# Strassen's scheme in the MLP of a two-block network: product order, order of the queues, and the engine that sums the quarters of u

## The chip, the cores and the metric

One core of a Trainium2 chip runs the whole network. The metric is the device time of one execution in microseconds (us), the median of several runs.

## The reference

The network has a first block (attention and a state-space mixer, one layer) and a second block of two layers, each a mixer followed by an MLP. The MLP is all that the change touches. It works on 512 tokens, with 1024 model columns and 4096 hidden columns:

```python
h = _rms_norm_2(x, g_pre_mlp[l])
y = jnp.square(jax.nn.relu(h @ w_up[l])) @ w_down[l]
x = x + _rms_norm_2(y, g_post_mlp[l])
```

All is float32. The kernel gets near float32 precision out of matmuls of rounded operands: each operand is split into a high part (a copy rounded to fp32r) and a low part (the operand minus the high part), and each product takes three matmuls, high by high, high by low, and low by high.

## The kernel before

The hidden columns are cut into 32 units of 128. `up(f)` makes unit f: 24 matmuls of 512 columns, then ACT takes the relu out of PSUM and squares it (`unit_done`). The result is called u.

The down product (u times `w_down`) of the first 24 units is done by a scheme of Strassen's: two units make a pair, and a 2x2 block product is made of 7 products instead of 8. The left side has four quarters of u (A11, A12, A22 in `U_ALL`, A21 in `A21_`) and four sums of them (S1 to S4, also in `U_ALL`). The right side has four quarters of the weights (B11, B21, B22 and B12) and four sums (T1 to T4, in `T_ALL`). One step is one pair against one half of the output columns: 7 products of 6 matmuls each, 42 matmuls of 256 columns. The last 8 units go the plain way.

The stage runs in 6 rounds a layer (d = 0 to 5), and each of the two layers has this stage. PE's order in round d is: step 0 (pair 2d), step 1 (pair 2d+1), `up(4d+5)`, step 2 (pair 2d), step 3 (pair 2d+1), `up(4d+6)`, `up(4d+7)`, `up(4d+8)`. The pair that step 1 needs is complete when `up(4d+3)` is, which is the last but one unit ahead of step 0 of the same round.

What is prepared for a step, and where:

- the sums T1 to T4 of the weights: DVE, `step_sums` (L531 to L533)
- high parts of the weights' quarters and of T: ACT, `step_hi` (L520, L521 for the quarters, then L523 for T, behind a wait for DVE's sums)
- low parts: DVE, `step_lo` (L540, L541) and `step_lo_sums` (L548)
- the sums S1 to S4 of u: POOL (L2701 to L2704, four operations on 128x256)
- high parts of u: ACT, `pair_hi` (L2320, the first 768 columns: A11, A12, A22) and `pair_hi_sums` (L2325, the 1024 columns of S1 to S4)
- low parts of u: POOL (L2708, two operations, of 768 and of 1024 columns)
- high and low part of the weights of `up`: ACT `up_hi` (L479) and DVE `up_lo` (L485)

A step on PE begins with two waits: for both low parts of the pair's u (`u_pool`), and for all parts of the step's weights (`w_lo`). The results of the products are added up on DVE by `collect` (L2564, L2567, out of PSUM) in seven tiles Z; at the end of the last round seven additions of 128x1024 (`plus`, L2594) make the output of them. Every engine works its queue in the order in which it is written; engines wait for one another by counting semaphores. `dve_link` and `pool_link` make an engine wait for its own operation just issued. The weights come by DMA in a ring of 8 slots, in PE's order, and a slot is loaded again when PE is done with it.

Of the kernel before, what the change touches and what calls it, by code (L numbers as in the profile page):

```python
# [62 lines left out]
def up_number(f):  # L63

    if f < 4:
        return J_MLP + f
    if f >= 4 * NST + 4:
        return J_LATE + f - 4 * NST - 4
    d, r = divmod(f - 4, 4)
    return J_MLP + 4 + 12 * d + (0, 3, 8, 11)[r]  # L70


def step_number(n):

    return J_MLP + 4 + 12 * (n // 4) + (1, 4, 6, 9)[n % 4]
# [9 lines left out]
PRODUCTS = ((A11, B11), (A12, B21), (S4, B22), (A22, T4), (S1, T1), (S2, T2), (S3, T3))  # L85
# [104 lines left out]
def build(nc, a, out, first=True, second=True):  # L190
# [20 lines left out]
    with ExitStack() as ctx:  # L211
# [76 lines left out]
        Z = [carve(A0, 2, 512), quarter(0, 0), quarter(0, 1), quarter(1, 0), quarter(1, 1), carve(A0 + 1024, 2, 512), carve(A0 + 2048, 2, 512)]  # L288
# [1890 lines left out]
        def two_act(act, l, post_gain):  # L2179
# [116 lines left out]
            def unit_done(f):  # L2296
# [13 lines left out]
                if p >= 2:  # L2310
                    act.wait_ge(sem.u_pool, N_POOL * l + 2 * (p - 2) + 1)
# [82 lines left out]
        def two_dve(dve, l):  # L2394
# [173 lines left out]

            for d in range(NST):
                if d:  # L2570
                    collect(d - 1, 1, range(7))
# [4 lines left out]
                up_lo(dve, l, 4 * d + 5)
                step_sums(dve, l, 4 * d + 1)
                step_lo(dve, l, 4 * d + 1)
                step_lo_sums(dve, l, 4 * d + 1)
# [70 lines left out]
        def two_pool(pool, l):  # L2650
# [286 lines left out]
```

## Time and profile before

| | |
|---|---|
| median of 3 runs | 1773.59 us (1771.93 to 1783.68) |
| profiled execution | 1772.09 us, span of its instructions 1770.0 us |
| mean granted clock of TensorE | 0.979 of full speed |
| PE busy | 1672.6 us, 94% of the span |
| DVE busy | 1114.7 us, 63% |
| ACT busy | 713.6 us, 40% |
| POOL busy | 564.8 us, 32% |

PE is TensorE's matmuls, DVE is VectorE, ACT is ScalarE, POOL is GpSimd. L and a number is a line of the kernel. The time of an execution is its span and some 2 us around it. A line of a timeline gives the start, the duration, the engine, the line, the operation, what it writes and reads, and, in brackets, how long the engine was idle before it and for whom it waited. A duration there reaches from the start of an operation to its end, and holds the time in which the operation itself was held up.

### The profile page before, as it was taken

The page shows a single profiled execution, that of the slowest core. Times are in us where ns is not written, and L with a number is a line of the kernel's source. Part 1 is how long each engine was busy: PE and PEld are TensorE (multiplying, and loading weights), DVE is VectorE, ACT ScalarE, POOL GpSimd, SP SyncE. Part 2 cuts the span into 40 slices and gives each one's busy share as a digit, 9 for nine tenths or more (in the row PEclk, how much of TensorE's full clock was granted, in tenths as well). Part 3 has the DMA queues.
Part 4 walks back from the last instruction along what each step waited for, and adds up shares of the span by engine and source line. Part 5 has one row for each costly group of instructions (what it writes and reads, how often), then busy time and mean ns, then how long its engine had stood idle before and what let it go on. Part 6 is the DMA issues. An engine that isn't in the chain of part 4 may idle for free.

```text
span 1770.0 us, 25358 instructions
## 1 busy us (share of the span) xinstructions
PE 1672.6 (94%) x9563; PEld 1303.7 (74%) x9563; DVE 1114.7 (63%) x1955; ACT 713.6 (40%) x1426; POOL 564.8 (32%) x594
## 2 busy tenths in 40 slices
PE   7989999999999999899999999999999989999998
PEld 4555456487866679888888778887667978888876
DVE  6999666345447735677777563444773577777754
ACT  3233342342346635443443244234672543343321
POOL 1010001231126635333333632112663533333360
PEclk9999999999999999999999999899999999999999
DMA  6324220145220005232323234422000522332321
GB/s 189 66 26 99 67 95 1 39 143 143 58 87 1 1 15 142 84 96 84 96 88 92 83 74 127 124 50 95 2 1 4 152 84 86 93 96 84 95 84 48
DMA packets 195019, 136.91 MB, mean 77 GB/s; under 512 B 34487, under 2 KB 176562, under 8 KB 194898
## 3 DMA queue, kind: packets, MB, share of 16 engines
q1 hardware_dynamic: 188604, 128.07, 24.8%
q10 hardware_dynamic: 6294, 7.22, 1.8%
q8 instruction: 77, 1.26, 0.3%
q14 instruction: 44, 0.36, 0.1%
HBM read 131.00 MB, written 2.10 MB: 75 GB/s over the span
## 4 chain that ended last, share of the span: by engine, by line
PE 73%; DVE 15%; ACT 4%; issue 3%; POOL 3%; DMA 2%; ACTq 0%; POOLq 0%; DVEq 0%; SPq 0%
PE ps L563 13%; PE ps L564 13%; PE ps L565 12%; PE ps L2115 4%; PE ps L2117 4%; PE ps L2116 4%; PE ps L1999 4%; PE ps L2015 3%; PE ps L2030 3%; PE ps L1199 3%; POOL U_LO L2708 1%; PE ps L1887 1%; DMA WR<-in_cmp_w_v 1%; PE ps L605 1%; DVE BIG L2594 1%
## 5 line engine op out<-in xcount | busy, mean ns | idle before, releaser
L565 PE MATMUL ps<-HT_R,WR_R 128*128 128x512 f32 (+1 forms) x832 | 314.1, 377 | 0.0
L563 PE MATMUL ps<-HT_R,UP_HI 128*128 128x512 f32 x448 | 178.7, 399 | 6.7 <-DVE WR_R L485 6.7
L565 PEld LDWEIGHTS ps<-HT_R,WR_R 128*128 128x128 f32 x832 | 157.5, 189 | 31.9
L564 PE MATMUL ps<-HL_MLP,UP_HI 128*128 128x512 f32 x448 | 178.0, 397 | 0.0
L485 DVE TENSOR_TENSOR WR_R<-WR,UP_HI 128x1024 fp32r<-128x1024 f32 x56 | 82.7, 1477 | 144.0 <-ACT UP_HI L479 143.9
L2187 ACT ACTIVATE BIG<-ps 64x512 f32<-64x512 f32 (+3 forms) x124 | 71.7, 580 | 180.7 <-PE ps L565 161.8
L2512 DVE CUSTOM_DVE_ANT_0 ps<-ps,tri 128x512 f32<-128x512 f32 (+1 forms) x192 | 93.1, 502 | 57.3 <-PE ps L1999 56.6
L2287 ACT ACTIVATE BIG<-ps,mn 128x512 f32<-128x512 f32 (+1 forms) x192 | 100.3, 528 | 59.9 <-DVE mn L2512 53.1
L2682 POOL TENSOR_SCALAR BIG<-BIG,rg,gate 128x512 f32<-128x512 f32 (+3 forms) x128 | 76.7, 613 | 149.2 <-DVE rg L2528 148.9
L2115 PE MATMUL ps<-H,U_HI 128*128 128x256 f32 x288 | 86.8, 301 | 39.5 <-POOL U_LO L2708 29.6
L2708 POOL TENSOR_TENSOR U_LO<-BIG,U_HI 128x768 fp32r<-128x768 f32 (+1 forms) x48 | 107.8, 2258 | 31.3 <-ACT U_HI L2325 29.4
L893 PE MATMUL ps<-WR,HT 128*128 128x512 f32 (+1 forms) x256 | 114.0, 596 | 1.2 <-ACT BIG L1676 1.2
L2115 PE MATMUL ps<-WH_MLP,U_HI 128*128 128x256 f32 x384 | 110.8, 289 | 0.0
L2116 PE MATMUL ps<-WH_MLP,U_HI 128*128 128x256 f32 x384 | 110.4, 288 | 0.0
L2117 PE MATMUL ps<-WH_MLP,U_LO 128*128 128x256 f32 x384 | 110.1, 287 | 0.0
L2701 POOL TENSOR_TENSOR BIG<-BIG 128x256 f32<-128x256 f32 x24 | 18.2, 759 | 287.6 <-ACT BIG L2308 287.6
L523 ACT ACTIVATE WH_MLP<-BIG 128x1024 fp32r<-128x1024 f32 x48 | 51.0, 1062 | 143.8 <-DVE BIG L533 143.8
L563 PEld LDWEIGHTS ps<-HT_R,UP_HI 128*128 128x128 f32 x448 | 85.0, 190 | 26.6 <-issue 7.5
L2567 DVE TENSOR_TENSOR BIG<-ps,BIG 128x512 f32<-128x512 f32 x140 | 93.4, 686 | 14.8 <-PE ps L2117 13.0
L564 PEld LDWEIGHTS ps<-HL_MLP,UP_HI 128*128 128x128 f32 x448 | 85.0, 190 | 18.6
L1999 PE MATMUL ps<-BIG 64*128 64x384 f32 (+7 forms) x384 | 96.9, 474 | 1.6 <-ACT BIG L2287 1.0
L564 PE MATMUL ps<-WR_R,HT_R 128*128 128x512 f32 (+1 forms) x256 | 95.0, 371 | 0.0
(398 smaller groups left out, 4304.2 us busy)
## 6 DMA issues: line engine op xcount, KB each, us to landing
WR<-in_w_up SPq DMA_DIRECT2D x64, 512.0 KB, 4.0
WR<-in_w_down SPq DMA_DIRECT2D x96, 256.0 KB, 3.3
WR<-in_w_in SPq DMA_DIRECT2D x36, 512.0 KB, 5.4
WR<-in_w_out SPq DMA_DIRECT2D x6, 2048.0 KB, 7.8
WR<-in_w_in SPq DMA_DIRECT2D x5, 2048.0 KB, 8.3
WR<-in_w_down SPq DMA_DIRECT2D x16, 512.0 KB, 3.6
WR<-in_cmp_w_k SPq DMA_DIRECT2D x2, 2048.0 KB, 8.2
WR<-in_cmp_w_v SPq DMA_DIRECT2D x2, 2048.0 KB, 8.2
```

What stands on the lines that cost most here:

```text
L563: nc.tensor.matmul(out_, w[0], x[0], start=start, stop=False)
L564: nc.tensor.matmul(out_, w[0], x[1], start=False, stop=False)
L565: return nc.tensor.matmul(out_, w[1], x[0], start=False, stop=stop)
L893: last = nc.tensor.matmul(ps[bank][:, 0:width], HT[:, k, P * m:P * m + P], wv[:, k, 0:width], start=(k == 0), stop=(k == KD - 1))
L1999: nc.tensor.matmul(s_bank(u, o)[:, 0:P * (t + 1)], q_of(kind, h, t), k_of(kind, h, P * (t + 1)), start=True, stop=True).then_inc(sem.s_ps, 1)
L2115: nc.tensor.matmul(out_, x[0], w[0], start=(i == 0 and t == 0), stop=False, skip_group_check=True)
L2116: nc.tensor.matmul(out_, x[0], w[1], start=False, stop=False, skip_group_check=True)
L2117: last = nc.tensor.matmul(out_, x[1], w[0], start=False, stop=(i == 1), skip_group_check=True)
L2287: nc.scalar.activation(PR[u % 3][:, o, 0:w], s_bank(u, o)[:, 0:w], ACT.Exp, bias=mn[:, i:i + 1], scale=-1.0, accum_out=rs[:, 2 * u + o:2 * ...
L2512: nc.vector.tensor_tensor_reduce(s_bank(u, o)[:, 0:w], s_bank(u, o)[:, 0:w], tri[:, SEQ - w:SEQ], 1.0, 3.0e38, ALU.add, ALU.min, mn[:, i:i ...
L2567: nc.vector.tensor_tensor(z, src, z, ALU.add).then_inc(sem.z_sum, 1)
L2708: last = nc.gpsimd.tensor_tensor(U_LO[p % 3][:, cols_], U_ALL[p % 3][:, cols_], U_HI[p % 3][:, cols_].bitcast(F32), ALU.subtract)
```

## The change

- Products: A22 by T4 comes third and S4 by B22 fourth (they change places), and the tiles Z are named to match.
- PE: the wait at the head of a step asks only for the first low part of u (A11, A12, A22) and for the low parts of the weights' quarters. The wait for T's low part stands ahead of the third product, the wait for the low part of S1 to S4 ahead of the fourth. POOL signals its two low parts one by one.
- S1 to S4 are computed by DVE (`pair_sums`) instead of POOL, in the same four operations. They stand between `step_lo_sums(4d)` and `step_sums(4d+1)` for the odd pair, between `step_lo_sums(4d+3)` and `up_lo(4d+7)` for the even one, and ahead of `step_sums(0)` for the first. They are counted by `t_sum`, which ACT and POOL now wait for.
- ACT: `up_hi(4d+5)` goes behind `step_hi(4d+1)` and `pair_hi_sums(2d+1)`. DVE: `up_lo(4d+5)` goes behind the sums and low parts of step 4d+1.
- End of the last round on DVE: the seven `plus` in another order, and `up_lo(28)` to `up_lo(31)` between them: 4 `plus`, 28, 1 `plus`, 29, 1 `plus`, 30, 1 `plus`, 31. Before: 28, 5 `plus`, 29, 2 `plus`, 30, 31.

```diff
-PRODUCTS = ((A11, B11), (A12, B21), (S4, B22), (A22, T4), (S1, T1), (S2, T2), (S3, T3))
+PRODUCTS = ((A11, B11), (A12, B21), (A22, T4), (S4, B22), (S1, T1), (S2, T2), (S3, T3))
...
             def strassen_step(d, sweep, i):
 
                 n, p = 4 * d + 2 * sweep + i, 2 * d + i
-                pe.wait_ge(sem.u_pool, N_POOL * l + 2 * p + 2)
-                pe.wait_ge(sem.w_lo, NSPLIT * l + step_number(n) + 2)
+                pe.wait_ge(sem.u_pool, N_POOL * l + 2 * p + 1)
+                pe.wait_ge(sem.w_lo, NSPLIT * l + step_number(n) + 1)
                 for q, (left, right) in enumerate(PRODUCTS):
                     if i == 0:
                         product_bank_free(d, sweep, q)
+                    if q == 2:
+                        pe.wait_ge(sem.w_lo, NSPLIT * l + step_number(n) + 2)
+                    if q == 3:
+                        pe.wait_ge(sem.u_pool, N_POOL * l + 2 * p + 2)
...
             def pair_hi_sums(p):
 
-                act.wait_ge(sem.u_pool, N_POOL * l + 2 * p + 1)
+                act.wait_ge(sem.t_sum, N_SUM * l + pair_sum_number(p))
...
                 pair_hi(2 * d + 1)
-                up_hi(act, l, c + 1)
                 step_hi(act, l, 4 * d + 1)
                 pair_hi_sums(2 * d + 1)
+                up_hi(act, l, c + 1)
                 unit_done(c)
...
+            def pair_sums(p):
+
+                part = lambda i: U_ALL[p % 3][:, 256 * i:256 * i + 256]
+                dve.wait_ge(sem.u_act, N_ACT * l + 5 * p + 3)
+                dve_link(nc.vector.tensor_tensor(part(S1), A21_[:, p % 2, :], part(A22), ALU.add))
+                dve_link(nc.vector.tensor_tensor(part(S2), part(S1), part(A11), ALU.subtract))
+                nc.vector.tensor_tensor(part(S3), part(A11), A21_[:, p % 2, :], ALU.subtract)
+                nc.vector.tensor_tensor(part(S4), part(A12), part(S2), ALU.subtract).then_inc(sem.t_sum, 1)
+
             for d in range(NST):
                 if d:
                     collect(d - 1, 1, range(7))
                 up_lo(dve, l, 4 * d + 4)
+                if d == 0:
+                    pair_sums(0)
                 step_sums(dve, l, 4 * d)
                 step_lo(dve, l, 4 * d)
                 step_lo_sums(dve, l, 4 * d)
-                up_lo(dve, l, 4 * d + 5)
+                pair_sums(2 * d + 1)
                 step_sums(dve, l, 4 * d + 1)
                 step_lo(dve, l, 4 * d + 1)
                 step_lo_sums(dve, l, 4 * d + 1)
+                up_lo(dve, l, 4 * d + 5)
...
+                if d + 1 < NST:
+                    pair_sums(2 * d + 2)
                 up_lo(dve, l, 4 * d + 7)
             collect(NST - 1, 1, range(7))
-            up_lo(dve, l, F_PLAIN + 4)
             dve.wait_ge(sem.z_sum, z_count(l, NST - 1, 1, 6))
             plus(1, 0)
-            plus(2, 4)
+            plus(3, 4)
             dve_link(plus(5, 0))
-            plus(2, 5)
+            plus(3, 5)
+            up_lo(dve, l, F_PLAIN + 4)
             dve_link(plus(6, 5))
             up_lo(dve, l, F_PLAIN + 5)
-            dve_link(plus(3, 6))
+            dve_link(plus(2, 6))
+            up_lo(dve, l, F_PLAIN + 6)
             dve_link(plus(4, 6))
-            for f in range(F_PLAIN + 6, NF):
-                up_lo(dve, l, f)
+            up_lo(dve, l, F_PLAIN + 7)
...
             for p in range(NPAIR):
-                pool.wait_ge(sem.u_act, N_ACT * l + 5 * p + 3)
-                pool_link(nc.gpsimd.tensor_tensor(part(S1), A21_[:, p % 2, :], part(A22), ALU.add))
-                pool_link(nc.gpsimd.tensor_tensor(part(S2), part(S1), part(A11), ALU.subtract))
-                nc.gpsimd.tensor_tensor(part(S3), part(A11), A21_[:, p % 2, :], ALU.subtract)
-                nc.gpsimd.tensor_tensor(part(S4), part(A12), part(S2), ALU.subtract).then_inc(sem.u_pool, 1)
-                pool.wait_ge(sem.u_pool, N_POOL * l + 2 * p + 1)
+                pool.wait_ge(sem.t_sum, N_SUM * l + pair_sum_number(p))
                 for n, cols_ in enumerate((slice(0, 768), slice(768, 1792))):
                     pool.wait_ge(sem.u_act, N_ACT * l + 5 * p + 4 + n)
-                    last = nc.gpsimd.tensor_tensor(U_LO[p % 3][:, cols_], U_ALL[p % 3][:, cols_], U_HI[p % 3][:, cols_].bitcast(F32),
-                                                   ALU.subtract)
-                last.then_inc(sem.u_pool, 1)
+                    nc.gpsimd.tensor_tensor(U_LO[p % 3][:, cols_], U_ALL[p % 3][:, cols_], U_HI[p % 3][:, cols_].bitcast(F32),
+                                            ALU.subtract).then_inc(sem.u_pool, 1)
```

## Rows read from the trace of the kernel before

**Rows 1.** Waits of PE over the whole span: us in total, times, longest us
```profile
PE ps L2115 <- POOL U_LO L2708: 29.6, 10, 3.0
PE ps L2115 <- DVE WH_MLP L548: 9.9, 2, 5.0
...
PE ps L563 <- DVE WR_R L485: 6.7, 2, 3.4
```

**Rows 2.** Busy time by stretch; its columns are in the first line
```profile
core 0: us, PE busy (x) PEld busy (x) DVE busy (x) ACT busy (x) POOL busy (x), PEclk, DMA share, GB/s
725.80:735.80 10.00, 10.00 (x86) 10.00 (x85) 6.50 (x8) 4.09 (x5) 8.12 (x6) 1.00 0.36 107
735.80:752.50 16.70, 16.70 (x74) 13.51 (x73) 7.53 (x11) 7.90 (x13) 3.38 (x4) 1.00 0.34 95
702.40:985.10 282.70, 262.92 (x1585) 235.75 (x1583) 207.98 (x251) 112.33 (x167) 108.63 (x78) 0.97 0.30 90
1411.90:1694.80 282.90, 263.14 (x1585) 236.04 (x1583) 208.01 (x251) 112.37 (x167) 108.58 (x78) 0.97 0.30 90
752.50:798.10 45.60, 42.64 (x265) 38.15 (x264) 33.61 (x43) 19.94 (x30) 16.65 (x13) 1.00 0.32 93
798.10:845.20 47.10, 44.14 (x265) 39.66 (x264) 33.79 (x43) 20.05 (x30) 16.66 (x13) 0.96 0.30 90
712.50:720.20 7.70, 7.70 (x43) 7.70 (x44) 6.42 (x11) 2.01 (x2) 0.00 (x0) 0.62 0.00 0
988.50:990.50 2.00, 1.98 (x5) 1.61 (x6) 1.97 (x2) 0.00 (x0) 1.92 (x2) 0.50 0.00 0
```

**Rows 3.** Timeline of PE, start of the second step of round 1
```profile
760.64 0.39 PE L2115 MATMUL ps<-H,U_HI 128*128 128x256 f32 x1 [2.96 <-POOL U_LO L2708]
```

**Rows 4.** Timeline of ACT, round 1 of layer 0
```profile
748.25 0.63 ACT L2308 ACTIVATE BIG<-relu 128x512 f32<-128x512 f32 x1
748.91 0.85 ACT L2320 ACTIVATE U_HI<-BIG 128x768 fp32r<-128x768 f32 x1
...
756.06 1.06 ACT L523 ACTIVATE WH_MLP<-BIG 128x1024 fp32r<-128x1024 f32 x1 [4.52 <-DVE BIG L533]
757.03 1.04 ACT L2325 ACTIVATE U_HI<-BIG 128x1024 fp32r<-128x1024 f32 x1
```

**Rows 5.** Timeline of DVE, round 1 of layer 0
```profile
747.77 1.23 DVE L548 TENSOR_TENSOR WH_MLP<-BIG,WH_MLP 128x1024 fp32r<-128x1024 f32 x1
...
753.61 1.96 DVE L532 TENSOR_TENSOR BIG<-WR,BIG 128x256 f32<-128x256 f32 x1
755.60 0.42 DVE L533 TENSOR_TENSOR BIG<-WR,BIG 128x256 f32<-128x256 f32 x1
...
757.15 1.23 DVE L548 TENSOR_TENSOR WH_MLP<-BIG,WH_MLP 128x1024 fp32r<-128x1024 f32 x1
...
772.10 1.22 DVE L548 TENSOR_TENSOR WH_MLP<-BIG,WH_MLP 128x1024 fp32r<-128x1024 f32 x1
```

**Rows 6.** Timeline of POOL, round 1 of layer 0
```profile
748.96 0.74 POOL L2701 TENSOR_TENSOR BIG<-BIG 128x256 f32<-128x256 f32 x1 [13.31 <-ACT BIG L2308]
...
753.10 2.19 POOL L2708 TENSOR_TENSOR U_LO<-BIG,U_HI 128x768 fp32r<-128x768 f32 x1
758.14 2.44 POOL L2708 TENSOR_TENSOR U_LO<-BIG,U_HI 128x1024 fp32r<-128x1024 f32 x1 [2.86 <-ACT U_HI L2325]
```

**Rows 7.** Timeline of ACT, second square of round 0
```profile
692.00 0.63 ACT L2308 ACTIVATE BIG<-relu 128x512 f32<-128x512 f32 x1
```

**Rows 8.** Timeline of DVE, low parts of round 0's second step
```profile
708.99 3.37 DVE L548 TENSOR_TENSOR WH_MLP<-BIG,WH_MLP 128x1024 fp32r<-128x1024 f32 x1
```

**Rows 9.** Timeline of POOL, first unit after the pairs, round 5
```profile
945.95 1.48 POOL L2714 TENSOR_TENSOR BIG<-BIG 128x512 f32<-128x512 f32 x1
```

**Rows 10.** Timeline of DVE, final sums of the products
```profile
976.76 9.63 DVE L2594 TENSOR_TENSOR BIG<-BIG 128x1024 f32<-128x1024 f32 x5
986.42 1.95 DVE L485 TENSOR_TENSOR WR_R<-WR,UP_HI 128x1024 fp32r<-128x1024 f32 x1
```

More of the change, by code:

```diff
@@ L58 @@
 N_ACT, N_POOL = 5 * NPAIR + NF - F_PLAIN, 2 * NPAIR + NF - F_PLAIN
+N_SUM = NSTEP + NPAIR
 J_LATE, J_DOWN = J_MLP + 4 + 12 * NST, J_MLP + 8 + 12 * NST
@@ L69, in up_number, with step_sum_number, pair_sum_number @@
     d, r = divmod(f - 4, 4)
-    return J_MLP + 4 + 12 * d + (0, 3, 8, 11)[r]
+    return J_MLP + 4 + 12 * d + (0, 5, 8, 11)[r]
 def step_number(n):
-    return J_MLP + 4 + 12 * (n // 4) + (1, 4, 6, 9)[n % 4]
+    return J_MLP + 4 + 12 * (n // 4) + (1, 3, 6, 9)[n % 4]
+def step_sum_number(n):
+    return 6 * (n // 4) + (1, 3, 4, 5)[n % 4] + 1
+def pair_sum_number(p):
+    return 3 * p - p % 2 + 1
 def relu_number(f):
@@ L287, in build @@
         quarter = lambda t, half: Y[:, 2 * t:2 * t + 2, 512 * half:512 * half + 512]
-        Z = [carve(A0, 2, 512), quarter(0, 0), quarter(0, 1), quarter(1, 0), quarter(1, 1), carve(A0 + 1024, 2, 512), carve(A0 + 2048, 2, 512)]
+        Z = [carve(A0, 2, 512), quarter(0, 0), quarter(1, 0), quarter(0, 1), quarter(1, 1), carve(A0 + 1024, 2, 512), carve(A0 + 2048, 2, 512)]
         HL_IN = [carve(17408, KD, SEQ), parts("HL_IN", at_BIG + 4 * 17408, KD, SEQ)]
@@ L521, in step_hi @@
             nc.scalar.activation(H2[i][:], WR[:, u.slot, 512:1024], ACT.Copy).then_inc(sem.w_hi, 1)
-            act.wait_ge(sem.t_sum, NSTEP * l + n + 1)
+            act.wait_ge(sem.t_sum, N_SUM * l + step_sum_number(n))
             nc.scalar.activation(WH_MLP[2 * i + 1][:], T_ALL[i], ACT.Copy).then_inc(sem.w_hi, 1)
@@ L537, in step_lo @@
             u, i = by_name[f"st{n}_{l}"], n % 2
-            dve.wait_ge(sem.t_sum, NSTEP * l + n + 1)
+            dve.wait_ge(sem.t_sum, N_SUM * l + step_sum_number(n))
             dve.wait_ge(sem.w_hi, NSPLIT * l + step_number(n) + 1)
@@ L2310, in unit_done @@
                 if p >= 2:
-                    act.wait_ge(sem.u_pool, N_POOL * l + 2 * (p - 2) + 1)
+                    act.wait_ge(sem.t_sum, N_SUM * l + pair_sum_number(p - 2))
                 if p >= 3:
@@ L2698, in two_pool @@
             for p in range(NPAIR):
-                part = lambda i: U_ALL[p % 3][:, 256 * i:256 * i + 256]
-                pool.wait_ge(sem.u_act, N_ACT * l + 5 * p + 3)
-                pool_link(nc.gpsimd.tensor_tensor(part(S1), A21_[:, p % 2, :], part(A22), ALU.add))
-                pool_link(nc.gpsimd.tensor_tensor(part(S2), part(S1), part(A11), ALU.subtract))
-                nc.gpsimd.tensor_tensor(part(S3), part(A11), A21_[:, p % 2, :], ALU.subtract)
-                nc.gpsimd.tensor_tensor(part(S4), part(A12), part(S2), ALU.subtract).then_inc(sem.u_pool, 1)
-                pool.wait_ge(sem.u_pool, N_POOL * l + 2 * p + 1)
+                pool.wait_ge(sem.t_sum, N_SUM * l + pair_sum_number(p))
                 for n, cols_ in enumerate((slice(0, 768), slice(768, 1792))):
                     pool.wait_ge(sem.u_act, N_ACT * l + 5 * p + 4 + n)
-                    last = nc.gpsimd.tensor_tensor(U_LO[p % 3][:, cols_], U_ALL[p % 3][:, cols_], U_HI[p % 3][:, cols_].bitcast(F32),
-                                                   ALU.subtract)
-                last.then_inc(sem.u_pool, 1)
+                    nc.gpsimd.tensor_tensor(U_LO[p % 3][:, cols_], U_ALL[p % 3][:, cols_], U_HI[p % 3][:, cols_].bitcast(F32),
+                                            ALU.subtract).then_inc(sem.u_pool, 1)
             for f in range(F_PLAIN, NF):
```

## The prediction

> **What bounds the kernel now.** I read the share of busy time first: PE is busy 94% of the span, the next engine 63%. So a gain can only come out of PE's idle time, or out of time in which PE runs at its low clock. The waits of PE say how much of it the change can reach [rows 1]: 29.6 us for POOL's low parts of u in 10 places, 9.9 us for a low part of T in 2 places, 6.7 us for the low part of an `up` weight in 2 places. That is 46.2 us. The third view is the table of stretches [rows 2]. It shows what the waits cost beyond themselves. Two steps without a wait between take 10.0 us and three `up` units 16.7 us, so a round of four steps and four units is worth 10.0 + 5.6 + 10.0 + 16.7 = 42.3 us (42.4 with the digits that the cut takes off). Round 1 takes 45.6 us with a wait of 3.0 us. Round 2 takes 47.1 us with the same wait: its granted clock is 0.96. The step behind the 5.0 us wait takes 7.7 us instead of 5.0, at a granted clock of 0.62. Half speed is TensorE's lower level, 1.2 instead of 2.4 GHz, and in each of these places PE had been idle just before the clock was down. So the waits are paid a second time.
>
> The whole prize: from the first step to the end of `up(28)` layer 0 takes 282.7 us and layer 1 282.9 us, against 6 x 42.4 = 254.4 us. That is 28.3 + 28.5 = 56.8 us. Behind it comes the wait of 3.4 us for `up_lo(29)` in each layer, with a clock of 0.50 in the 2 us after it [rows 1, 2], worth some 1.2 us more: 2 x 4.6 = 9.2 us. Together 66 us can be had at most.
>
> **Why PE waits in a round.** Times are from the start of round 1's step 0 at 752.5. The square that completes pair 3 ends at -3.6 [rows 4]. POOL starts the sums 0.1 us later, and is done with its first low part at +2.8. Its second waits until +5.6 for ACT, and ends at +8.1 [rows 6]; PE starts step 1 there, 3.0 us late [rows 3]. ACT was late because its copy of T stands ahead of the copy of S and waited for DVE's last sum of T, done at +3.5 [rows 4, 5]. DVE was late because `up_lo(4d+5)` stood ahead of these sums, and because it was held: a sum of 256 columns takes 0.42 us, but the one at 753.61 took 1.96 us. It ended at 755.57, 0.3 us behind the end of POOL's operation that began at 753.10 [rows 5, 6]. Operations of DVE and POOL that read two SBUF tensors keep each other out.
>
> **The change part by part.**
>
> *The sums of u on DVE.* Four operations of 0.42 us with two links between are 1.7 us; POOL took 0.74 us for one alone and 4.1 us for all (748.96 to 753.10). DVE is free at -3.5 (L548 ends at 749.0 [rows 5]) and the square is there, so nothing is waited for: sums done at -1.8. DVE goes on with the first sum of T (0.7 us), to -1.2. POOL's first low part takes 1.9 us alone, until +0.7. DVE's other two sums end at +1.6. ACT's copies of T and of S (1.06 and 1.04 us) end at +2.7 and +3.6. DVE's `step_lo` ends at +2.5 and `step_lo_sums` (1.23 us) at +3.9. POOL's second low part waits for this and takes 2.44 us: +6.4 instead of +8.1.
>
> *The waits inside the step.* Step 1 may begin at +5.0. It needs the first low part (+0.7) and the quarters' (+2.5). A product takes 5.0 / 7 = 0.72 us: the third comes at +6.4 and needs T (+3.9), the fourth at +7.2 and needs +6.4. So no wait is left, by a margin of 0.8 us. Added waits that are met already cost nothing that can be seen: a step with a wait in front of every product and one with none take 10.0 us together, 84 matmuls at an even pace [rows 2]. If the pair's part had to be complete at the head, as before, 1.4 us would remain.
>
> *`up_hi` and `up_lo(4d+5)` later.* ACT makes the high part until +4.7, DVE the low part when POOL lets go, +6.4 to +7.6; PE needs it at +10.0.
>
> *What is late next.* PE comes 3.1 us earlier to the later steps, DVE doesn't. Before, the last low part of step 3 was ready at 773.3, +20.8 [rows 5]; in the new order `step_sums(4d+2)` ends at +9.2 in place of +9.5, so it comes at +20.5. Step 3 now begins at 10.0 + 5.6 + 5.0 = +20.6 and wants T at +22.0. It fits, by 1.5 us. The even pair's sums (1.7 us) follow on DVE at +20.5, ahead of `up_lo(4d+7)` (ready about +25.8 with POOL in between, wanted at +31.2) and of the seven sums of products, whose first is wanted at +31.2 and done near +26.4. In round 5 POOL also has the unit behind the pairs: it asks for the port as soon as the pair is done (1.48 us for its first operation [rows 9], three operations in all). This can push DVE back 2 to 3 us, so that step 3 there waits 1 us: -1 us a layer.
>
> *Round 0.* The square of pair 0 ends at 692.6 [rows 7]. The same walk gives the second low part of u at 702.6, in time for step 0 at 702.4. Then ACT has two units to square (2.5 us), DVE starts pair 1's sums behind POOL at 702.6, and the parts for step 1 come at 708.7 (quarters), 710.1 (T; before, 712.4 [rows 8]), 712.5 (low part of S). PE is ready at 707.4: it waits 1.3 us at the head and 1.7 us at the fourth product. For the clock I take 1.5 us, as behind the 3.0 us wait of round 2 (bounds 0 and 2.7, the rows of rounds 1 and 0). This leaves 4.5 us a layer.
>
> *The end.* Five `plus` took 9.63 us, 1.93 each, and `up_lo(29)` stood behind them (986.42 to 988.37, PE ready at 985.1) [rows 10]. With four ahead of `up_lo(28)`, DVE starts them 0.9 us after step 3's end and does `up_lo(28)` 9.8 us after it; PE wants it at 11.2. `up_lo(29)` is done by 14.5 and wanted at 16.8; the later ones wait for ACT as before. The wait goes, with its clock: 4.6 us a layer.
>
> Sum: 56.8 + 9.2 - 2 x 4.5 - 2 x 1 = 55 us. Profiled execution: 1772.1 - 55 = 1717. The median of before is 1.5 us above it: 1718.5 us.
>
> **A rule against the row.** The gap between 1.96 and 0.42 us for one and the same sum is what I put down to POOL. The Trainium skill, Advanced Engine Details, section "VectorE Performance Modes", lets only DVE's 2-port modes clash with POOL, and these sums (float32, two SBUF inputs) would not be among them; the same skill's SBUF — State Buffer, section "Who interferes with whom", says that two SBUF inputs are enough, and the row sides with that. By the first rule alone the sums of round 0's step 1 would not be held, which is the first rival below.
>
> **The rivals.**
>
> *No exclusion.* What the row shows is then chance. In round 0 the sums would end at 703.9 and the second low part of u at about 710.0, wanted at 709.5: 0.5 us in place of 4.5, and none in round 5. 8 + 2 us less: 1708.5. The row speaks against it, and so do its neighbours. 4%.
>
> *The second low part of u misses the fourth product.* My margin there is 0.8 us in a chain of ten operations and handovers. If POOL is let in one operation of DVE later (1.2 us), or two, each of the 10 rounds keeps 0.5 to 1.5 us, in half of them with 1 us of clock: 10 to 20 us given back, 1728 to 1739. 24%.
>
> *DVE becomes the bound, and it is slower.* DVE is busy 33.6 us of round 1 [rows 2]; 3.4 us come on top, and POOL's two low parts of both pairs, 8.6 us, shut out its SBUF work: 45.6 us at worst against the 42.4 that PE wants. At both `pair_sums` it also stands still until ACT's square, with `step_sums` or `collect` queued behind, and PE waits for those. At 1.5 us for each stand the round takes 48.6 us, 2 more than the present mean of some 46.6: 11 rounds, +22 us, 1795. It decides from stands of 0.5 us on. Against it: the 33.6 holds time in which DVE was held by POOL already, and its sums out of PSUM (L2567) do not read two SBUF tensors. 3%.
>
> *The time is given back at step 2 or 3.* If the later steps' parts are as late as before and PE only meets them sooner, the 3.1 us move to step 3. My walk has 1.5 us of margin at T. If it is wrong by 3, only the end and round 0 gain: 1760. 7%.
>
> **How the numbers follow.** Forecast 1718.5, 58%, own range 1708 to 1726 (clock of round 0 between its bounds, the 2 us of round 5 gone or doubled). A measurement here tells about 1% from nothing. With 4% left for what I see no case for (half of it between 1739 and 1756), faster by over 1% (below 1755.9) holds 0.89, within 1% 0.07, slower 0.04. For 8 in 10 the range takes in the better rival and the misses of the fourth product: 1706 to 1740.
>
> **What would show it.** Right: no wait of PE for L2708's successor in rounds 1 to 5; rounds of 42.4 us; a wait of about 3 us in two parts at round 0's step 1; S1 to S4 on DVE at 0.42 us each when POOL is still; no wait for `up_lo(29)`; DVE's busy time up by 24 x 1.7 = 41 us less what it was held before, POOL's down by up to 24 x 4.1 = 98 us. Wrong: a wait ahead of the fourth product in every round (second rival), PE waiting at steps 2 and 3 for `step_lo_sums`, or a first low part of u that does not begin until DVE's sums of T are done and pushes the second behind +7.2.

## The result and the profile after

The changed kernel takes 1714.25 us (median of 4 runs, 1707.73 to 1719.12) against 1772.76 us (4 runs, 1768.89 to 1783.68): a ratio of 0.9658, 95% interval 0.9604 to 0.9712. The forecast was 1718.5 us. The profiled execution took 1707.73 us, 64.4 us less than that of before; its span is 1705.8 us. It is the fastest of the four executions of the changed kernel, while the profiled one of before lies near its median; so the medians differ by less, 58.5 us.

PE's idle time first, from the page of the changed kernel (line of engines):

```profile
PE 1649.0 (97%) x9563; PEld 1283.3 (75%) x9563; DVE 1127.8 (66%) x2051; ACT 711.0 (42%) x1426; POOL 482.5 (28%) x498
```

and PE's waits in it (us in total, times, longest us). The step's matmuls are now at L2130 to L2132, `up` at L574 to L576:

```profile
PE ps L2130 <- POOL U_LO L2731: 2.1, 2, 1.1
...
PE ps L2130 <- DVE WR_R L552: 0.5, 2, 0.3
```

These are all the waits in the steps that PE's list still shows. The 29.6, 9.9 and 6.7 us of [rows 1] have become 2.1 and 0.5 us, all in round 0. The table of stretches, for the six rounds of each layer up to `up(28)`, rounds 1 and 2, the first two steps of round 0, and the units and last additions behind the rounds:

```profile
core 0: us, PE busy (x) PEld busy (x) DVE busy (x) ACT busy (x) POOL busy (x), PEclk, DMA share, GB/s
702.30:958.10 255.80, 254.47 (x1585) 228.45 (x1584) 217.85 (x296) 112.77 (x170) 72.70 (x34) 1.00 0.34 99
1379.50:1635.30 255.80, 254.47 (x1585) 228.50 (x1584) 217.89 (x296) 112.77 (x170) 72.64 (x34) 1.00 0.34 99
746.40:788.70 42.30, 42.30 (x265) 38.05 (x264) 35.49 (x51) 19.77 (x30) 9.90 (x5) 1.00 0.34 100
788.70:831.10 42.40, 42.40 (x266) 38.08 (x266) 35.57 (x51) 19.77 (x30) 10.01 (x5) 1.00 0.34 100
702.30:714.10 11.80, 10.47 (x86) 10.09 (x85) 10.85 (x14) 6.51 (x12) 4.70 (x2) 1.00 0.29 89
941.40:974.90 33.50, 33.50 (x146) 27.02 (x145) 19.70 (x17) 8.69 (x11) 23.08 (x15) 1.00 0.31 94
```

The six rounds take 255.8 us in place of 282.7 and 282.9 [rows 2]. Rounds 1 and 2 take 42.3 and 42.4 us, all of it busy, at full clock: 45.6 and 47.1 before, and the 42.4 us that four steps and four units are worth. The granted clock is 1.00 in every row: in this execution the low clock went with the waits. That is the smaller part of the gain. PE's waits in the steps and for `up_lo(29)` fell by 46.2 - 2.6 = 43.6 us; in the stretch defined below, which was 63.6 us shorter, PE was also busy 20.1 us less, with the same matmuls.

The chain that used to be late, in round 1 (step 0 begins at 746.42). DVE:

```profile
742.82 0.43 DVE L2588 TENSOR_TENSOR BIG<-BIG 128x256 f32<-128x256 f32 x1
743.28 0.42 DVE L2589 TENSOR_TENSOR BIG<-BIG 128x256 f32<-128x256 f32 x1
743.74 0.42 DVE L2590 TENSOR_TENSOR BIG<-BIG 128x256 f32<-128x256 f32 x1
744.08 0.42 DVE L2591 TENSOR_TENSOR BIG<-BIG 128x256 f32<-128x256 f32 x1
744.41 0.69 DVE L542 TENSOR_TENSOR BIG<-WR 128x512 f32<-128x512 f32 x1
745.13 1.95 DVE L543 TENSOR_TENSOR BIG<-WR,BIG 128x256 f32<-128x256 f32 x1
747.12 0.42 DVE L544 TENSOR_TENSOR BIG<-WR,BIG 128x256 f32<-128x256 f32 x1
...
748.67 1.23 DVE L559 TENSOR_TENSOR WH_MLP<-BIG,WH_MLP 128x1024 fp32r<-128x1024 f32 x1
```

ACT and POOL:

```profile
742.15 0.63 ACT L2323 ACTIVATE BIG<-relu 128x512 f32<-128x512 f32 x1
...
747.58 1.06 ACT L534 ACTIVATE WH_MLP<-BIG 128x1024 fp32r<-128x1024 f32 x1 [3.09 <-DVE BIG L544]
748.54 1.05 ACT L2340 ACTIVATE U_HI<-BIG 128x1024 fp32r<-128x1024 f32 x1
```

```profile
744.58 2.23 POOL L2731 TENSOR_TENSOR U_LO<-BIG,U_HI 128x768 fp32r<-128x768 f32 x1 [12.74 <-DVE BIG L2591]
749.66 2.50 POOL L2731 TENSOR_TENSOR U_LO<-BIG,U_HI 128x1024 fp32r<-128x1024 f32 x1 [2.86 <-ACT U_HI L2340]
```

DVE begins the sums of u as soon as the square has ended (742.78), has them at 744.50, goes on with T's first sum, and its second (745.13) is held until POOL's first low part lets go: 1.95 us, as in [rows 5]. POOL's second low part ends at 752.16, 5.7 us after the start of step 0. The fourth product of step 1 wants it at 7.2.

Read over both layers, the time from the first matmul of step 0 of round 0 to the first matmul of the plain down product fell from 304.3 + 304.6 = 608.9 us to 272.65 + 272.67 = 545.3 us: 63.6 of the 64.2 us of span. I call this the MLP stretch below. It is the sharper measure: in the profiles of all kernels here this stretch began between 699.2 and 711.4 us after the start, with the same instructions ahead of it, while the two layers of one profile agree within 0.1 us where no low clock falls, and within 1.6 us elsewhere. It rests on one profiled execution of each kernel, so for kernels with low clock in it a difference of some 2 us says nothing.

### The profile page after: what moved, and what is told of

Same layout as the page of the kernel before. It is cut to its first block, busy times and chain, and to the rows that moved or that the text cites. A ratio compares the mean times of both kernels' runs of the same rounds, so it can differ in the third digit from the quotient of the medians.

```text
span 1705.8 us, 25404 instructions
## 1 busy us (share of the span) xinstructions
PE 1649.0 (97%) x9563; PEld 1283.3 (75%) x9563; DVE 1127.8 (66%) x2051; ACT 711.0 (42%) x1426; POOL 482.5 (28%) x498
## 4 chain that ended last, share of the span: by engine, by line
PE 79%; DVE 13%; issue 2%; ACT 2%; DMA 2%; POOL 2%; ACTq 0%; DVEq 0%; POOLq 0%; SPq 0%
PE ps L574 14%; PE ps L575 14%; PE ps L576 14%; PE ps L2130 4%; PE ps L2131 4%; PE ps L2132 4%; PE ps L2010 4%; PE ps L2026 3%; PE ps L2041 3%; PE ps L1210 3%; PE ps L1898 1%; DMA WR<-in_cmp_w_v 1%; PE ps L616 1%; PE ps L1118 1%; PE ps L1199 1%
## 5 line engine op out<-in xcount | busy, mean ns | idle before, releaser
L576 PE MATMUL ps<-HT_R,WR_R 128*128 128x512 f32 (+1 forms) x832 | 313.3, 377 | 0.0
L2731 POOL TENSOR_TENSOR U_LO<-BIG,U_HI 128x768 fp32r<-128x768 f32 (+1 forms) x48 | 118.2, 2472 | 357.3 <-DVE BIG L2591 317.3
L576 PEld LDWEIGHTS ps<-HT_R,WR_R 128*128 128x128 f32 x832 | 156.9, 189 | 31.7
L574 PE MATMUL ps<-HT_R,UP_HI 128*128 128x512 f32 x448 | 177.3, 396 | 0.0
L496 DVE TENSOR_TENSOR WR_R<-WR,UP_HI 128x1024 fp32r<-128x1024 f32 x56 | 106.3, 1898 | 80.3 <-ACT UP_HI L490 79.1
L2131 PE MATMUL ps<-WH_MLP,U_HI 128*128 128x256 f32 x384 | 108.3, 282 | 0.0
L2132 PE MATMUL ps<-WH_MLP,U_LO 128*128 128x256 f32 x384 | 108.3, 282 | 0.0
L2130 PE MATMUL ps<-WH_MLP,U_HI 128*128 128x256 f32 x384 | 108.3, 282 | 0.0
L574 PEld LDWEIGHTS ps<-HT_R,UP_HI 128*128 128x128 f32 x448 | 84.2, 188 | 19.0
L904 PEld LDWEIGHTS ps<-WR,HT 128*128 128x128 f32 x256 | 48.5, 194 | 56.0 <-issue 54.5
L2582 DVE TENSOR_TENSOR BIG<-ps,BIG 128x512 f32<-128x512 f32 x140 | 87.0, 677 | 0.0
L2130 PE MATMUL ps<-H,U_HI 128*128 128x256 f32 x288 | 81.4, 283 | 2.7 <-POOL U_LO L2731 2.1
```

The source lines that it names most:

```text
L496: nc.vector.tensor_tensor(lo, whole, hi.bitcast(F32), ALU.subtract).then_inc(sem.w_lo, 1)
L574: nc.tensor.matmul(out_, w[0], x[0], start=start, stop=False)
L576: return nc.tensor.matmul(out_, w[1], x[0], start=False, stop=stop)
L904: last = nc.tensor.matmul(ps[bank][:, 0:width], HT[:, k, P * m:P * m + P], wv[:, k, 0:width], start=(k == 0), stop=(k == KD - 1))
L2130: nc.tensor.matmul(out_, x[0], w[0], start=(i == 0 and t == 0), stop=False, skip_group_check=True)
L2131: nc.tensor.matmul(out_, x[0], w[1], start=False, stop=False, skip_group_check=True)
```

## The experiments

Four parts of the change can be set apart: S, the sums of u on DVE; Q, `up_hi` and `up_lo(4d+5)` behind step 4d+1's work; W, the waits inside the step with the product order; E, the order at the end of the last round. Three kernels take S, Q or W out of the changed one (E was not taken out), four put one part alone into the kernel before. All seven keep the new product order, also those without W: what the order is worth by itself was not measured. The trace lets me estimate it. With S4 by B22 third, the second low part of u is wanted at 6.4 us, and it is there at 5.7: nothing in rounds 1 to 5, and some 0.7 us more of wait in round 0. The kernel before ran beside them at medians of 1767.5 to 1772.8 us.

**head_waits: W taken out**

```diff
                 for q, (left, right) in enumerate(PRODUCTS):
-                    if q == 2:
-                        pe.wait_ge(sem.w_lo, NSPLIT * l + step_number(n) + 2)
-                    if q == 3:
-                        pe.wait_ge(sem.u_pool, N_POOL * l + 2 * p + 2)
```

and both waits for the full counts at the head.

> The changed kernel with both waits of a step back at its head (both low parts of u, and T's low part), all else as changed. Walk of the queues: the second low part of u is ready 5.8 us after step 0 begins and PE could start step 1 at 5.0, so PE waits 0.8 us at the head of step 1 in rounds 1 to 5, and some 3.8 us in round 0 of each layer. 10 x 0.8 + 2 x (3.8 - 1.3) = 13 us more than the changed kernel, with low clock behind the waits up to 10 us more: 1727 to 1737 us. Rival, that the in-step waits are of no use because sums and queue order did all: 1714 us, no wait in rounds 1 to 5.

Measured: 1731.5 us, ratio to before 0.9792 (0.9757 to 0.9827); MLP stretch 563.3 us, 18.0 more than the changed kernel. PE waits 0.63 us in each of rounds 1 to 5 (0.8 expected) and 3.7 us in round 0, where the granted clock of the first two steps is 0.79 in one layer and 0.89 in the other. The time is in the range expected. The rival is out: without W the step waits in every round. Of the 18.0 us some 8.2 are round 0, 9.0 the other rounds' steps 0 and 1.

**old_queues: Q taken out**

```diff
                 pair_hi(2 * d + 1)
+                up_hi(act, l, c + 1)
                 step_hi(act, l, 4 * d + 1)
                 pair_hi_sums(2 * d + 1)
-                up_hi(act, l, c + 1)
...
                 pair_sums(2 * d + 1)
+                up_lo(dve, l, 4 * d + 5)
                 step_sums(dve, l, 4 * d + 1)
                 step_lo(dve, l, 4 * d + 1)
                 step_lo_sums(dve, l, 4 * d + 1)
-                up_lo(dve, l, 4 * d + 5)
```

> The changed kernel with up_hi and up_lo of unit 4d+5 back in front of the sums and splits of step 4d+1. Walk: DVE waits for up_hi, then its low part (1.2 us), then T's sums around POOL's first low part; the second low part of u is ready at 7.7 us, the fourth product wants it at 7.2: a wait of 0.6 us at the fourth product in rounds 1 to 5. 1720 to 1728 us. Rival, that the parts add up one by one, each worth a third of the 3.0 us wait: a wait of 1.0 us in each round, 1724 to 1735 us.

Measured: 1720.05 us, ratio 0.9716 (0.9686 to 0.9746); MLP stretch 550.7 us, 5.4 more. Steps 0 and 1 of a later round take 10.25 us instead of 9.99: the second low part of u ends at 7.2 us, where it is just wanted, so the wait is under 0.3 us where 0.6 was expected. The rival's 1.0 us is out. Of the 5.4 us 3.0 are round 0. So W covers nearly all that Q would give.

**pool_sums: S taken out** (`u_pool` counts three a pair then: the sums and the two low parts; DVE's `pair_sums` goes)

```diff
             for p in range(NPAIR):
-                pool.wait_ge(sem.t_sum, N_SUM * l + pair_sum_number(p))
+                pool.wait_ge(sem.u_act, N_ACT * l + 5 * p + 3)
+                pool_link(nc.gpsimd.tensor_tensor(part(S1), A21_[:, p % 2, :], part(A22), ALU.add))
+                pool_link(nc.gpsimd.tensor_tensor(part(S2), part(S1), part(A11), ALU.subtract))
+                nc.gpsimd.tensor_tensor(part(S3), part(A11), A21_[:, p % 2, :], ALU.subtract)
+                nc.gpsimd.tensor_tensor(part(S4), part(A12), part(S2), ALU.subtract).then_inc(sem.u_pool, 1)
```

> The changed kernel with the four sums of u back on POOL, in-step waits and new queue order kept. Walk: POOL's four sums and DVE's three sums of T want the port in turn, so T's sums end 0.2 us after step 0 begins and the first low part of u at 3.2 us; T's low part waits behind the second low part of u (3.9 to 6.3 us) and is ready at 7.6 us; the third product wants it at 6.4: a wait of 1.2 us ahead of the third product in rounds 1 to 5. 1727 to 1738 us. Rival, that DVE is 1.7 times as fast as POOL and this alone is what counts: a wait of 2.4 us (4.1 - 1.7) in each round, 1738 to 1755 us.

Measured: 1710.71 us, ratio 0.9674 (0.9644 to 0.9705). Both theories were wrong: no wait in rounds 1 to 5. By the time of the whole it can't be told from the changed kernel. The MLP stretch is 547.5 us, 2.2 more, all of it in round 0 (0.9 us a layer) and at step 3 of round 5 (0.2 us). In round 1 of it (step 0 at 746.08), DVE and POOL:

```profile
742.47 0.68 DVE L542 TENSOR_TENSOR BIG<-WR 128x512 f32<-128x512 f32 x1
743.19 0.85 DVE L543 TENSOR_TENSOR BIG<-WR,BIG 128x256 f32<-128x256 f32 x1
744.08 0.85 DVE L544 TENSOR_TENSOR BIG<-WR,BIG 128x256 f32<-128x256 f32 x1
...
746.88 2.88 DVE L559 TENSOR_TENSOR WH_MLP<-BIG,WH_MLP 128x1024 fp32r<-128x1024 f32 x1
```

```profile
742.52 1.24 POOL L2716 TENSOR_TENSOR BIG<-BIG 128x256 f32<-128x256 f32 x1 [10.74 <-ACT BIG L2323]
743.84 0.81 POOL L2717 TENSOR_TENSOR BIG<-BIG 128x256 f32<-128x256 f32 x1
744.72 0.80 POOL L2718 TENSOR_TENSOR BIG<-BIG 128x256 f32<-128x256 f32 x1
745.48 0.92 POOL L2719 TENSOR_TENSOR BIG<-BIG 128x256 f32<-128x256 f32 x1
746.48 5.53 POOL L2723 TENSOR_TENSOR U_LO<-BIG,U_HI 128x768 fp32r<-128x768 f32 x2
```

Each engine's sums slip in between the other's: DVE's take 0.85 us instead of 0.42, and T's are done at 744.93, 1.15 us ahead of step 0. In the changed kernel they are done 1.12 us behind it (747.12 + 0.42), because POOL, freed of the sums, starts its long first low part in their middle. POOL's sums end 2.2 us later than DVE's did, but POOL never waits for ACT: both its low parts run through (746.48 + 5.53) and end 5.9 us after step 0 begins, against 5.7. My walk had put T's low part behind the second low part of u; it went ahead (749.76).

**round0: an attempt at a faster version**

```diff
-                if d == 0:
-                    pair_sums(0)
                 step_sums(dve, l, 4 * d)
+                if d == 0:
+                    pair_sums(0)
...
+                if d == 0:
+                    step_sums(dve, l, 1)
                 pair_sums(2 * d + 1)
-                step_sums(dve, l, 4 * d + 1)
+                if d:
+                    step_sums(dve, l, 4 * d + 1)
```

> The changed kernel with step_sums(0) ahead of pair_sums(0), and step_sums(1) ahead of pair_sums(1), in round 0 of each layer alone: DVE is idle 7.8 and 2.1 us ahead of these sums of u, and the sums of T need nothing of u. The sums of T no longer meet POOL's low part. The 1.33 us of PE's waits in round 0 go in each layer: 2.7 us less than the changed kernel, 1711.5 us; the stretch of the six rounds shrinks from 255.5 to 254.2 us. Rival, that ACT's squares set round 0: the waits stay, 1714 us.

The counts that `t_sum` waits for are changed to match. Measured: 1706.5 us (median of 6), ratio 0.9658 (0.9628 to 0.9687), the same ratio as the changed kernel's; MLP stretch 543.7 us, 1.6 less (2.7 expected). The stretch tells it apart, the time of the whole doesn't. Of the 1.33 us of waits 0.75 us came back in another place: POOL's two low parts now follow without a gap and hold DVE's low parts of the second step. DVE and POOL in round 0:

```profile
700.74 2.35 DVE L552 TENSOR_TENSOR WR_R<-WR,H 128x512 fp32r<-128x512 f32 x1
703.01 3.43 DVE L559 TENSOR_TENSOR WH_MLP<-BIG,WH_MLP 128x1024 fp32r<-128x1024 f32 x1
```

```profile
700.56 4.79 POOL L2734 TENSOR_TENSOR U_LO<-BIG,U_HI 128x768 fp32r<-128x768 f32 x2 [4.28 <-DVE BIG L2591]
```

**waits_only, sums_only, queues_only, end_only: one part alone in the kernel before**

The edits are those shown, each on top of the new product order (W; `pair_sums` on DVE ahead of `up_lo(4d+5)`; the two moves; the order of `plus`).

> The kernel before with the product order and the in-step waits alone (POOL signals each low part). Walk on the rows of before: the second low part of u is ready 8.1 us after step 0 begins, the fourth product wants it at 7.2: PE waits 1.0 us instead of 3.0 in rounds 1 to 5. 10 x 2.0 us, some of the low clock (0 to 1.1 a round) and 1 to 3 us of round 0: 1738 to 1750 us. Rival, that the parts add up, a third each: wait of 2 us, 1755 to 1763.

> The kernel before with the sums of u on DVE alone, ahead of up_lo(4d+5); waits at the head, old queue order, old end. Walk: the second low part of u is ready at 7.7 instead of 8.1 us, PE waits 2.7 instead of 3.0 us: 1763 to 1771 us. Rival, a third each: wait of 2 us, 1755 to 1763.

> The kernel before with the new place of up_hi and up_lo of unit 4d+5 alone; sums of u on POOL, waits at the head, old end. Walk: T's low part comes last, at 7.6 us instead of 8.1 for u: PE waits 2.6 instead of 3.0 us: 1762 to 1770 us. Rival, a third each: wait of 2 us, 1755 to 1763.

> The kernel before with the new order of the seven last additions and up_lo(28) to (31) alone. The wait of 3.4 us for up_lo(29) and 1.2 us of low clock go in each layer: 9 us less, 1764 us. The additions took 1.93 us each; if POOL held them, those that begin before POOL's next unit take less, as in the changed kernel (1.19 us). Rival, that the wait moves to up_lo(28): 1769 us.

Measured, with those above (the wait is PE's at step 1 in rounds 1 to 5):

| kernel | parts | median us | ratio to before | wait us | MLP stretch us |
|---|---|---|---|---|---|
| before | none | 1772.76 | | 3.0 | 608.9 |
| end_only | E | 1756.49 | 0.9923 (0.9896 to 0.9950) | 3.0 | 596.6 |
| sums_only | S | 1758.59 | 0.9911 (0.9882 to 0.9940) | 2.1 | 593.8 |
| queues_only | Q | 1744.73 | 0.9833 (0.9792 to 0.9873) | 0.8 | 575.7 |
| waits_only | W | 1737.47 | 0.9796 (0.9758 to 0.9833) | 0.85 | 568.9 |
| head_waits | S Q E | 1731.5 | 0.9792 (0.9757 to 0.9827) | 0.6 | 563.3 |
| old_queues | S W E | 1720.05 | 0.9716 (0.9686 to 0.9746) | under 0.3 | 550.7 |
| pool_sums | Q W E | 1710.71 | 0.9674 (0.9644 to 0.9705) | 0 | 547.5 |
| changed | all | 1714.25 | 0.9658 (0.9604 to 0.9712) | 0 | 545.3 |

The lines of PE's waits, for Q alone, W alone and S alone:

```profile
PE ps L2126 <- POOL U_LO L2719: 17.1, 12, 4.6
```

```profile
PE ps L2130 <- POOL U_LO L2723: 8.5, 10, 0.9
...
PE ps L2130 <- DVE WR_R L552: 3.3, 2, 1.7
PE ps L2130 <- DVE WH_MLP L559: 3.2, 2, 1.6
```

```profile
PE ps L2126 <- POOL U_LO L2727: 31.0, 12, 5.2
```

W alone came out as walked (0.85 us against 1.0; 1737.5 us against 1738 to 1750). Q alone did far better than my 2.6 us and 1762 to 1770 us, for the reason seen in pool_sums: with the sums of u on POOL and no `up_lo` between, T's sums slip in between them. S alone did better than my 2.7 us and 1763 to 1771 us: a wait of 2.1 us. There POOL's first low part held `up_lo` instead of T's sums, as DVE's lines show in round 1 of sums_only:

```profile
749.99 2.86 DVE L496 TENSOR_TENSOR WR_R<-WR,UP_HI 128x1024 fp32r<-128x1024 f32 x1 [0.15 <-ACT UP_HI L490]
752.78 0.68 DVE L542 TENSOR_TENSOR BIG<-WR 128x512 f32<-128x512 f32 x1
```

The rival that each part gives a third fails for Q alone (0.8 us), W alone (0.85 us) and old_queues. S alone, by itself, came out as that rival had it (2.1 us against 2, 1758.6 us in its 1755 to 1763); as a rule for the three parts it is out. Alone the parts save 15.1 (S), 33.2 (Q), 40.1 (W) and 12.3 us (E) of the MLP stretch, 100.7 in sum; together 63.6 (low clock moves each of the four by some 2 us). Three of them shorten one wait, and it can go only once. Taken out last, W is worth 18.0 us, Q 5.4 and S 2.2.

E alone saved more than the 9 us expected: 9.8 us behind the rounds (33.5 us a layer from the end of step 3 to the down product, 38.4 before), the other 2.5 us inside them, where the waits are the same and nearly all of the difference is how often the low clock fell (six of the ten rounds 1 to 5, seven before; the first two steps of round 0 took 16.6 and 17.1 us in the two layers, 17.8 and 16.5 before). So E is worth 9.8 us, and the rest is luck. The first four additions run in 4.75 us:

```profile
976.76 4.75 DVE L2604 TENSOR_TENSOR BIG<-BIG 128x1024 f32<-128x1024 f32 x4
```

**twice_low: the margin at the fourth product**

```diff
                     pool.wait_ge(sem.u_act, N_ACT * l + 5 * p + 4 + n)
+                    if n:
+                        pool_link(nc.gpsimd.tensor_tensor(U_ALL[p % 3][:, cols_], U_ALL[p % 3][:, cols_],
+                                                          ones[:, 0:1].to_broadcast([P, 1024]), ALU.mult))
```

> The changed kernel with one more operation of POOL ahead of the second low part of u of every pair: the same 1024 columns times 1.0, written back (the result is the same). It measures the margin at the fourth product. In the changed kernel the second low part is ready 5.7 us after step 0 begins and wanted at 7.2, a margin of 1.4 us. Walk: with 2.5 us more it is ready at 8.2, PE waits 1.0 us in rounds 1 to 5 and 2.5 us more in round 0, and no wait appears at steps 2 and 3: 10 x 1.0 + 2 x 2.5 = 15 us and up to 8 us of low clock: 1729 to 1737 us. Rival, that margins elsewhere are the narrower ones because POOL holds DVE: waits at steps 2 and 3 for T's low parts too, over 1740 us.

Measured: 1749.1 us, ratio 0.9891 (0.9857 to 0.9926), 12 us above the range expected, and inside the rival's; but the waits that the rival names are not there. Rounds 1 to 5 are near the walk: a wait of 1.30 us in each, no wait at steps 2 and 3. So the margin is real, and the rival's mechanism is out. Round 0 was not near the walk: the two pairs' operations pile up on POOL, PE waits 2.25 and 3.85 us. The stretch with the second wait, and the one behind it:

```profile
718.80:725.00 6.20, 2.37 (x18) 2.17 (x18) 5.52 (x3) 3.81 (x7) 5.18 (x2) 0.93 0.15 50
725.00:730.30 5.30, 5.28 (x24) 5.28 (x25) 5.23 (x10) 2.00 (x2) 0.00 (x0) 0.50 0.00 0
```

3.85 us idle, then 5.3 us at 0.50. Per layer round 0 costs 7.4 us more, the other rounds 7.8. That makes 30.3 us of the MLP stretch (575.6 us); the medians differ by 4.6 us more, which lie outside it, and nothing in the traces ties them to the edit.

**twice_sums: is DVE near its bound?**

```diff
                 dve.wait_ge(sem.u_act, N_ACT * l + 5 * p + 3)
+                dve_link(nc.vector.tensor_tensor(part(S1), A21_[:, p % 2, :], part(A22), ALU.add))
+                dve_link(nc.vector.tensor_tensor(part(S2), part(S1), part(A11), ALU.subtract))
+                nc.vector.tensor_tensor(part(S3), part(A11), A21_[:, p % 2, :], ALU.subtract)
+                dve_link(nc.vector.tensor_tensor(part(S4), part(A12), part(S2), ALU.subtract))
                 dve_link(nc.vector.tensor_tensor(part(S1), A21_[:, p % 2, :], part(A22), ALU.add))
```

The four lines that follow are those of the changed kernel.

> The changed kernel with DVE's four sums of u done twice for every pair (the same results). It asks whether DVE is near to being the bound. Each pair costs DVE 1.8 us more, 3.6 us a round, and the chain to step 1 gets 1.8 us longer: the second low part of u is ready at 7.5 us, wanted at 7.2. Walk: a wait of 0.4 us in rounds 1 to 5, 1.8 us more in round 0, none at steps 2 and 3: 1721 to 1725 us. Rival, DVE as the bound: each round grows by the full 3.6 us less its idle time, over 1750 us.

Measured: 1721.37 us, ratio 0.9742 (0.9700 to 0.9784). PE's waits:

```profile
PE ps L2130 <- DVE WR_R L552: 9.4, 4, 3.7
...
PE ps L2130 <- POOL U_LO L2735: 2.2, 10, 0.2
```

0.2 us in rounds 1 to 5; the 9.4 us are round 0 (3.7) and step 3 of round 5 (1.06) in each layer. Round 0's first two steps take 3.7 and 4.5 us more than in the changed kernel where 1.8 was expected: the granted clock there is 0.89 and 0.79. 3.6 us more of DVE's time a round cost PE 0.5 us: DVE is not the bound, except in round 5, where it has the least to spare.

**low_after_t: who holds whom**

```diff
-                pool.wait_ge(sem.t_sum, N_SUM * l + pair_sum_number(p))
+                pool.wait_ge(sem.t_sum, N_SUM * l + (step_sum_number(2 * p - 1) if p % 2 else pair_sum_number(p)))
```

> The changed kernel, with POOL's first low part of the odd pairs waiting for T's sums of step 4d+1 instead of the sums of u that stand just ahead of them on DVE. Theory, that DVE and POOL shut each other out of SBUF for whole operations: DVE's second sum of T (L543 of the changed kernel, 1.95 us in rounds 1 to 5) takes 0.42 us in every round, POOL's low part starts 0.6 us later than the sums end now allow and holds DVE's low parts instead; the second low part of u is ready near 5 us, the time is the changed kernel's or 1 us less, 1712 to 1715 us. Rival, no exclusion: L543 keeps its 1.95 us.

Measured: 1718.69 us, ratio 0.9707 (0.9665 to 0.9749), 4 us above the range expected; MLP stretch 546.9 us. In round 1 of it (step 0 at 752.65), DVE and POOL:

```profile
751.35 0.42 DVE L543 TENSOR_TENSOR BIG<-WR,BIG 128x256 f32<-128x256 f32 x1
...
752.61 2.34 DVE L552 TENSOR_TENSOR WR_R<-WR,H 128x512 fp32r<-128x512 f32 x1
754.87 3.43 DVE L559 TENSOR_TENSOR WH_MLP<-BIG,WH_MLP 128x1024 fp32r<-128x1024 f32 x1
```

```profile
752.31 4.91 POOL L2731 TENSOR_TENSOR U_LO<-BIG,U_HI 128x768 fp32r<-128x768 f32 x2 [14.95 <-DVE BIG L544]
```

The held sum is free: 0.42 us. What POOL's operation now meets is held instead: 2.34 and 3.43 us for operations that take 0.69 and 1.23. The exclusion is shown. The hold only moved. The second low part of u ends at 4.6 us (near 5 expected), and of the 1.5 us more of the stretch 1.3 are waits in round 0, for these low parts above all, and 0.2 come at step 3 of round 5. The profiled span is 10.7 us longer than the changed kernel's. The other 9 us lie outside the stretch, which ran at a granted clock of 1.00, while the mean of the whole is 0.983 against 0.992.

## Why the prediction was right, step by step

- *The bound and the prize.* Confirmed. The prize was put at 66 us, 63.6 us of the MLP stretch were won, 43.6 of them waits and the rest mostly clock.
- *Rounds 1 to 4.* No wait is left, as forecast. The second low part of u ends at 5.7 us (forecast 6.4), because the chain ran 0.4 us ahead of my walk up to T's low part (749.90, +3.5, forecast +3.9) and POOL's operation took 2.3 us behind it: margin 1.4 us instead of 0.8. If the waits had stayed at the head, 1.4 us were to remain: 0.63 were measured.
- *The sums of u on DVE.* 0.42 us each and done at -1.9 (forecast 0.42 and -1.8): the duration and the place were right. What I did not ask is what the same change would do without them. It does nearly the same, 2.2 us of 63.6, since POOL then meets DVE with short operations instead of a long one. The forecast rested on the walk of all parts together, so this did not touch it.
- *Round 5.* Forecast 1 us of wait at step 3, measured 0.1: the last low part of step 3 ended 21.7 us after the round's start, wanted at 22.0. The mechanism is there (DVE's three sums took 1.52, 0.71 and 1.40 us), the cost was set too high.
- *Round 0.* The mis-sized term. Forecast waits of 1.3 and 1.7 us and 1.5 us of clock; measured 0.27 and 1.06 us and no low clock, 11.8 us for the first two steps instead of 10.0 at best. ACT's two squares ended at 701.7 instead of 702.2, and DVE began pair 1's sums then, 0.9 us ahead of the walk. The quarters' low parts came at 707.5 (forecast 708.7), T's at 708.8 (710.1) and that of S at 711.1 (712.5), and behind waits this short no low clock fell. 4.5 us a layer were forecast, 1.8 came: this and round 5 are 7.2 of the 8.6 us between the 55 us forecast and the 63.6 won in the stretch.
- *The end.* No wait for an `up` weight, as forecast; from the end of step 3 to the down product 33.5 us, 38.4 before: 4.9 a layer against 4.6 forecast. Part of this was luck, since two errors cancelled. DVE starts the additions 2.3 us behind the end of step 3 (941.4), forecast 0.9, because it is still busy with the sums of products. But the first four took 1.19 us each and not the 1.93 of [rows 10]: POOL was idle here until 947.84, while before it worked beside them. `up_lo(28)` is done 9.0 us behind the end of step 3 (forecast 9.8):

```profile
943.66 4.75 DVE L2622 TENSOR_TENSOR BIG<-BIG 128x1024 f32<-128x1024 f32 x4
948.74 1.66 DVE L496 TENSOR_TENSOR WR_R<-WR,UP_HI 128x1024 fp32r<-128x1024 f32 x1 [0.32 <-ACT UP_HI L490]
950.32 1.63 DVE L2622 TENSOR_TENSOR BIG<-BIG 128x1024 f32<-128x1024 f32 x1
954.40 1.23 DVE L496 TENSOR_TENSOR WR_R<-WR,UP_HI 128x1024 fp32r<-128x1024 f32 x1 [2.46 <-ACT UP_HI L490]
```

POOL in the changed kernel, and in the kernel before while the additions of [rows 10] ran:

```profile
947.84 1.48 POOL L2736 TENSOR_TENSOR BIG<-BIG 128x512 f32<-128x512 f32 x1 [6.55 <-ACT BIG L2317]
```

```profile
977.40 2.15 POOL L2717 TENSOR_TENSOR uT_lo<-BIG,uT_hi 128x512 fp32r<-128x512 f32 x1
```

- *The rivals.* No exclusion: out (low_after_t). Second low part too late: did not happen, and twice_low shows that it would have cost about 1.5 us a round for 2.5 us of delay. DVE as the bound: out (twice_sums). Given back at steps 2 and 3: out.
- *The busy times.* DVE's rose by 13.1 us (forecast 41 less what it had been held), POOL's fell by 82.3 (forecast up to 98).

The median of the changed kernel, 1714.25 us, is 4 us below the forecast. That this is so close is partly luck: for the profiled execution 1717 us was forecast, and 1707.73 came. The other three executions of the changed kernel took 5 to 11 us more, at mean clocks of 0.982 to 0.985 against 0.992. There is no trace of them; low_after_t shows that such low clock can lie outside the MLP stretch. PE's two waits of round 0 are these:

```profile
707.69 0.35 PE L2130 MATMUL ps<-H,U_HI 128*128 128x256 f32 x1 [0.27 <-DVE WR_R L552]
...
711.12 0.39 PE L2130 MATMUL ps<-H,U_HI 128*128 128x256 f32 x1 [1.06 <-POOL U_LO L2731]
```

## What to carry to other kernels

Several fixes of one wait do not add up. Walk each of them alone and all but one, since the part that looks largest (here the move to the faster engine, 15.1 us alone and 2.2 us as the last one) can be the one that the others make needless. When a wait can be taken inside a group of matmuls, at the first product that needs the operand, try that first: here it won 40.1 us by itself, more than either part that made the operand earlier (33.2 and 15.1 us). Where two engines shut each other out, ask which operations will meet, and not only which engine is faster: with the sums on the slower engine T's sums were done earlier (pool_sums), since they met short operations instead of a long one.

## What the runs showed of the hardware that I had not expected

- How PE's clock answered to waits. Behind waits of 0.6 to 1.3 us in rounds 1 to 5 (head_waits, queues_only, waits_only, twice_low) the first two steps took longer by the wait and 0.3 us. This is no low clock: the granted clock of the two steps is 1.00 in head_waits, and part of the 0.3 us is the way of counting, since a wait is counted from the end of a matmul of 0.28 us, and matmuls start every 0.12 us. Behind 2.1 us two rounds of ten lost 1.5 us more (sums_only), at a granted clock of 0.88; behind 3.0 us seven of ten did in the kernel before and six of ten in end_only. Behind 3.85 us the next 5.3 us ran at 0.50 (twice_low). The length of the wait does not settle it: the same wait of 3.0 us cost 1.5 us of clock in one round and none in another.
- DVE and POOL take turns, one operation each, when both have work ready (pool_sums, also queues_only). A short operation that meets a short one takes 0.85 us on DVE (0.42 alone) and 0.80 on POOL (0.74); behind a long one it is held for as long as the long one runs (1.95 us in place of 0.42 in the changed kernel).
